# Windowed attention: the scores of block i+3 issued between the transposes of block i and its products with v

## The reference

```
logits = q @ k.T - slope * |distance|, masked beyond a distance of 128 (at most 384 keys)
m = max(max(logits), sink);  p = exp(logits - m)
probs = p / (sum(p) + exp(sink - m));  out = probs @ v
```

## Time and profile before

| | |
|---|---|
| median of 3 runs | 2577.83 us (2577.28 to 2594.84) |
| the profiled execution | 2581.01 us |
| its span, first to last instruction | 2579.1 us |
| TensorE busy | 2317.2 us, 90% |
| VectorE busy | 1866.5 us, 72% |
| ScalarE busy | 1545.5 us, 60% |
| GpSimd busy | 318.4 us, 12% |
| mean granted clock of TensorE | 0.953 |

### The profile page before, as it was taken

One profiled execution on the slowest core, in us unless ns is written; L12 is line 12 of the kernel. 1 busy time (PEld: TensorE's weight loads), 2 busy tenths in 40 slices (PEclk: granted clock), 3 DMA queues, 4 the chain that ended last, 5 costly groups with the idle time before them and its releaser, 6 DMA issues. The chain is left out here.

```text
span 2579.1 us, 34366 instructions
## 1 busy us (share of the span) xinstructions
PE 2317.2 (90%) x11432; PEld 1756.2 (68%) x11432; DVE 1866.5 (72%) x2481; ACT 1545.5 (60%) x2032; POOL 318.4 (12%) x260
## 2 busy tenths in 40 slices
PE   7899989679999999939999999998967999999991
PEld 5666658657777777727788888876855777777770
DVE  5775582578898898848566676556257988988984
ACT  5554461448778778725555565546044877877872
POOL 0000020012122122130000000003001222212213
PEclk9999999879999999969999999999988999999996
DMA  3013011479999999852000000002147999999985
GB/s 123 26 38 115 25 65 41 174 252 403 398 398 404 396 399 405 348 170 98 25 25 24 24 24 12 12 24 69 38 174 262 401 401 400 404 396 398 402 341 216
DMA packets 129964, 538.51 MB, mean 209 GB/s; under 512 B 23696, under 2 KB 52496, under 8 KB 80752
## 3 DMA queue, kind: packets, MB, share of 16 engines
q1 hardware_dynamic: 110960, 470.66, 47.7%
q0 software_dynamic: 18944, 67.12, 7.4%
HBM read 487.54 MB, written 50.20 MB: 208 GB/s over the span
## 5 line engine op out<-in xcount | busy, mean ns | idle before, releaser
L1535 DVE TENSOR_TENSOR m_lo_gate<-m_raw_gate,m_hi_gate 128x2048 fp32r<-128x2048 f32 x132 | 296.7, 2289 | 87.1 <-ACT m_hi_gate L1530 85.0
L1535 DVE TENSOR_TENSOR m_lo_up<-m_raw_up,m_hi_up 128x2048 fp32r<-128x2048 f32 x128 | 292.2, 2283 | 0.1
L1535 DVE TENSOR_TENSOR m_lo_down<-m_raw_down,m_hi_down 128x2048 fp32r<-128x2048 f32 x124 | 278.1, 2284 | 0.0
L1530 ACT CAST m_hi_down<-m_raw_down 128x2048 fp32r<-128x2048 f32 x124 | 236.1, 1905 | 44.7 <-PEq L863 26.8
L1530 ACT CAST m_hi_up<-m_raw_up 128x2048 fp32r<-128x2048 f32 x128 | 244.1, 1908 | 7.1 <-DMA m_raw_up<-in_moe_w_up_dram 7.1
L1530 ACT CAST m_hi_gate<-m_raw_gate 128x2048 fp32r<-128x2048 f32 x132 | 245.1, 1906 | 0.0
L1539 POOL DMA_INDIRECT m_xg<-hn_rows,m_pick x62 | 183.7, 2963 | 390.4 <-PE m_XT L1662 388.8
L1649 PE MATMUL m_G<-m_hi_gate,m_x_hi 128*96 128x512 f32 x512 | 205.2, 401 | 16.0 <-DVE m_x_lo L1759 16.0
L1649 PE MATMUL m_U<-m_hi_up,m_x_hi 128*96 128x512 f32 x512 | 205.2, 401 | 0.0
L1650 PE MATMUL m_G<-m_hi_gate,m_x_lo 128*96 128x512 f32 x512 | 205.0, 400 | 0.0
L1651 PE MATMUL m_G<-m_lo_gate,m_x_hi 128*96 128x512 f32 x512 | 202.9, 396 | 0.0
(11 more groups left out here) (379 smaller groups left out, 4982.8 us busy)
## 6 DMA issues: line engine op xcount, KB each, us to landing
m_raw_gate<-in_moe_w_gate_dram SPq DMA_DIRECT2D x128, 1024.0 KB, 9.3
m_raw_up<-in_moe_w_up_dram SPq DMA_DIRECT2D x128, 1024.0 KB, 11.7
m_raw_down<-in_moe_w_down_dram SPq DMA_DIRECT2D x124, 1024.0 KB, 10.2
out_rows<-m_y POOLq DMA_DIRECT2D x64, 384.0 KB, 8.0
a1n_rows<-in_diff_w_qkv_dram SPq DMA_DIRECT2D x21, 512.0 KB, 5.5
out_rows<-a0n_gain SPq DMA_DIRECT2D x1, 8064.0 KB, 37.1
x_res<-in_x_dram SPq DMA_DIRECT2D x4, 1024.0 KB, 9.7
a0n_rows<-in_swa_w_o_dram SPq DMA_DIRECT2D x8, 512.0 KB, 3.2
```

The costliest lines, as they stand in the source:

```text
L1530: act.copy(self.hi[w][:, cut], self.raw[w][:, cut]).then_inc(self.hi_done[w], 1)
L1535: eng.tensor_tensor(self.lo[w][:, cut], self.raw[w][:, cut], self.hi[w][:, cut].bitcast(F32), ALU.subtract)\
```

## The change

In `product(i)` the scores of block i+3 are issued between the first two transposes and the first product with v. The loop no longer issues head_scores(i+2) ahead of product(i); head_scores(2), which stood there for i = 0, now stands ahead of the loop, in the same place of TensorE's order. The instructions are the same in kind and number; the waits stand with them. VectorE's, ScalarE's and GpSimd's orders are as before.

```diff
                         turn(0)
                         turn(1)
+                        if i + 3 < NT:
+                            head_scores(i + 3)
                         if i >= 2:
                             pe.wait_ge(oT_ready, n - 1)
                         times_v(0)
...
                     head_scores(1)
                     value_rows(1)
+                    head_scores(2)
+                    pe.wait_ge(v_rows_ready, 2 * g + 2)
                     for i in range(NT):
-                        if i + 2 < NT:
-                            head_scores(i + 2)
-                        if i == 0:
-                            pe.wait_ge(v_rows_ready, 2 * g + 2)
                         product(i)
```

## The result

The changed kernel took 2602.84 us (median of 10 runs, 2592.62 to 2613.36), the kernel before 2579.01 us (median of 10, 2576.04 to 2594.84). The ratio is 1.0077, 95% interval 1.0050 to 1.0103: slower by 0.8%, as forecast (+0.78%, 2598, range 2587 to 2608). This ratio goes by all runs and lies near that of the means (2602.64 and 2582.55 us, 20.1 us apart); the two medians are 23.8 us apart. The profiled execution took 2592.62 us, the shortest of the ten.

The account below looks back on a forecast made before the run. TensorE was taken to bound the block. Sweeps +16.9, product(0) +1.0 and clock +2.1 gave +20.0 us on 2577.83, rounded 2598 us, range 2587 to 2608.

Parts of the forecast that it names:

- The added wait: Products 1 to 4: scores wait for VectorE's mask behind heads_out, a closed chain of 6.93 us a block.
- product(4): Groups 0 to 2: the weights' low part adds 1.26 us between heads_out and mask, making 8.13 us, plus clock loss.
- The clock term: product(4) of groups 0 to 2: idle time lowers TensorE's clock, 1.5 us each, +4.6 us (0 to 4.6).
- Group 3: Last group's sweep, without low part: 27.66 us against 26.22, taken with GpSimd's interference as +2.0 us (1.4 to 3.3).
- my allowance for GpSimd's interference: Last group's sweep: GpSimd delays heads_out, 0 to 0.45 us more in each of 4 blocks.
- product(0) and the tail: product(0): scores cost +1.0 us (0 to 2), clock gains -1.5 and -1.0 in groups 2 and 3; products 5 to 7: 0.
- Sum of the stage: All terms of the attention together: +20.0 us, from 16.9 in the sweeps, 1.0 in product(0) and 2.1 of clock.
- What a sweep gains or loses should pass to the end unchanged: Whole span: all stages run one after the other, so the sweeps' loss reaches the total in full.
- The first (faster): Inside product(i): masks finish before the transposes end, scores fill 0.45 us a block, total 2568 us; chance 0.07.
- The second: Sweeps: the same chain, but the clock holds and the tail wins a little, +13.4 us, 2591 us; chance 0.25.
- The fourth (nothing passes to the end): After the sweeps: projections or DMA absorb the longer sweep, no change, 2578 us; chance 0.04.
- The third: New blocks: TensorE's clock falls in most, +10 us over half of them (2608), +20 over all (2618); chance 0.12.

Follow-up runs that it names:

- e1: Changed kernel with VectorE's heads_out(i-2) placed after masked_scores(i+1), TensorE's order as changed: 2591.05 us, ratio 0.9996 to the kernel before.
- e4: Changed kernel with the scores of block i+3 later in the product, between turn(2) and times_v(1), for i = 1 to 4: 2592.21 us, ratio 1.0018.
- e7: Kernel before with VectorE's heads_out(i-2) placed after masked_scores(i+1), nothing changed on TensorE: 2594.49 us, ratio 1.0040.
- e2: Changed kernel with the weights' low part behind masked_scores(6) on VectorE in place of ahead of it: 2602.36 us, ratio 1.0056.
- e3: Changed kernel with the scores of block 7 back ahead of product(5), so that product(4) carries none: 2606.98 us, ratio 1.0077.
- e5: Changed kernel with two VectorE alterations, heads_out(i-2) after masked_scores(i+1) and the low part after masked_scores(6): 2603.26 us, ratio 1.0045.

## Why the prediction was right, and where only its total was

- **The added wait: right.** A closed chain of 6.93 us a block was forecast from five rows, 6.80 was measured: heads_out 0.14 after the end (0.15 said), the first mask 0.89 later (0.89), head 3 after 2.05 (2.05), the product 0.46 after it (0.52), its end after 3.26 (3.33). e1 cut the chain on VectorE and the wait vanished; e4 let the same masks finish first and it vanished too; e7 shows that VectorE's order alone is worth nothing.
- **product(4): right in kind.** 8.13 us plus 1.5 of clock was said, 8.97 to 9.55 measured; e2 gave 1.26 + 1.27 us a group for low part and clock. The clock term was 3.8 us over three groups where 4.6 was said.
- **Group 3: mis-sized.** +2.0 was said, +0.79 measured. Half of the miss is my allowance for GpSimd's interference, 0.56 us, which was not needed; the other half is that the blocks took 6.7 to 6.8 us in place of 6.93. Before, they were already 6.25 to 6.94.
- **product(0) and the tail: mis-sized.** +1.0 and -2.5 were said, together -1.5; outside the sweeps the stage changed by 13.7 - 17.75 = -4.0. In product(0) the scores cost 0.1 us in groups 0 and 1, and 1.1 and 1.2 us were won in groups 2 and 3: -2.2. From product(4) to the end of a group, where I had taken 0, 0.1, 0.7, 0.1 and 0.4 us were won, 1.4 together. The last 0.4 lies in the first group's projections, where the half-clock stretch was shorter.
- **Sum of the stage:** +20.0 said, +13.7, +17.0 and +13.9 in three profiles. The mechanism was right and the sum 3 to 6 us too large. Against the first profile the 6.3 us are 1.2 in blocks 1 to 3 (6.80 for 6.93), 1.4 in product(4), most of it clock, 1.2 in group 3, 0.7 in product(0), and 1.8 in the tails and projections. One reading was off without effect on the sum: ScalarE's exponentials end at 92.34, as the 0.48 us ahead of the copy in the earlier trace rows say, not at 92.7.
- **"What a sweep gains or loses should pass to the end unchanged": right for like with like,** since runs at the same step differ by 15 to 20 us. e2 and e3, with stages 8.3 and 10.0 us over the kernel before, lie 10 to 15 us over it in runs of like granted clock. But the ratio of 1.0077, or +19.9 us, agrees with my +20.0 partly by chance: 14 to 17 us of it are stage, and the rest, as far as the clocks of the runs tell, is how many executions of each kernel lost a routing stage; by the medians the change cost 23.8 us. The reverse holds less well: e1's stage is 4.9 us shorter than before, its runs of like granted clock only 1.7 and 0.5 us. My prediction priced the clock only inside the attention and did not see that the remainder holds steps as large as the whole effect.
- **Rivals.** The first (faster) failed as its condition said: the first scores start 87.20 - 85.55 = 1.65 us after the product's end, and the transposes take 0.9. The second, with the clock holding and a small win in the tail, had +13.4 us: near the 13.7 and 13.9 us of two stages, but by another way, since the clock did fall in product(4). The fourth (nothing passes to the end) failed with the total. The third, a clock that falls in most blocks, did not come: all blocks 1 to 3 at 6.80. The Trainium skill, TensorE: Matmul & The Clock Gate, section "A second HAM failure mode: psum-queue depth-cycling", describes a clock that swings when TensorE idles briefly between groups of matmuls; blocks 1 to 3 idle 0.78 us each and did not show it. Only in product(4), after 2.04 us, did the clock fall, once in each of groups 0 to 2.

**Left open:** whether a longer or shorter attention stage changes how often a routing stage stays at 1.2 GHz. By totals and mean clocks the kernel before never lost both in its runs (none above 2599 us), while e5 did in seven of twelve (2603 to 2609 us) and e7, with a stage as long as before, in three of twelve, all with the same code in between. An edit to the routing stages would have to test it; none was tried.

## What to carry to other kernels

Before an instruction is moved forward on its engine, find the last instruction on the other engine that must release it, and read what stands ahead of that one in its own order. Here TensorE's scores moved by one block, VectorE's heads_out did not, and a wait that had a block of slack became a circle through both engines. Moved together (e1), the same edit shortens the block from 5.9 to 5.4 us in groups 0 to 2; and where the totals come in steps, compare the stage, and runs of like granted clock, not the median alone.

## What was not expected of the hardware

In a routing stage of e1 TensorE was busy for 20.00 of 20 us and stayed at a granted clock of 0.50 through the whole stretch, while the same code in the kernel before was busy 18.8 of 20 us and kept 1.00. The Trainium skill, TensorE: Matmul & The Clock Gate, section "What's actually happening", says that activity lifts the throttle; in these rows the stretch with the fuller busy time is the one at the lower level, so here the busy share did not tell which level was granted. Whether a routing stage stood at the one level or the other made some 15 us, as much as the whole edit added to the stage.
